# Products with the values for two query heads at once, in a decoder block's attention

## The reference, cut to what matters

```python
N_HEADS = 8; N_KV_HEADS = 2; GQA = 4; HEAD_DIM = 64
WINDOW = 512; Q_BLOCK = 128; SEL_BLOCK = 64; SEL_TOPK = 16
...
s_s = jnp.einsum('bqhgd,bhqsd->bhgqs', qc, ks).astype(f32) * scale + bias_s
p_s = _masked_softmax(s_s, (dist_s >= 0)[:, :, None])
o_s = jnp.einsum('bhgqs,bhqsd->bqhgd', p_s.astype(dtype), vs)
...
s_w = jnp.einsum('bqhgd,bkhd->bhgqk', qc, kw).astype(f32) * scale + bias_w
p_w = _masked_softmax(s_w, valid_w)
o_w = jnp.einsum('bhgqk,bkhd->bqhgd', p_w.astype(dtype), vw)
...
o = g[..., 0:1] * o_cmp + g[..., 1:2] * unblock(o_sel) + g[..., 2:3] * unblock(o_win)
x = x + jnp.concatenate([y_ssm, y_attn], axis=-1) @ w_out[l]
```

## Time and profile before

| | |
|---|---|
| Median of 3 runs | 1084.52 us (1084.23 to 1085.79) |
| Profiled execution | 1085.15 us, its span 1083.3 us |
| TensorE busy | 999.2 us, 92% |
| VectorE busy | 485.3 us, 45% |
| ScalarE busy | 278.5 us, 26% |
| Attention stage | 372 to 597 us of the span |
| Mean granted clock of TensorE | 0.963 of 2.4 GHz |

### The profile page before, as it was taken

How to read it: one execution, slowest core, us unless ns; L and a number is a source line. 1 busy time by engine, 2 the same in 40 slices (tenths; PEclk the granted TensorE clock), 3 DMA queues, 4 the chain that set the end, 5 groups by cost and what they waited for, 6 DMA issues and landing times. The chain is left out here.

```text
span 1083.3 us, 13456 instructions
## 1 busy us (share of the span) xinstructions
PE 999.2 (92%) x5091; PEld 583.5 (54%) x5091; DVE 485.3 (45%) x1213; ACT 278.5 (26%) x629; POOL 149.9 (14%) x146
## 2 busy tenths in 40 slices
PE   6998899989999899999999999996999888989991
PEld 4434687766555466767667455564454333434440
DVE  3444595078635367666665224264651111212115
ACT  3200111131222477656655111020011000101024
POOL 4000000031211212110010000011022101112230
PEclk9999899999999999999999999995999989999996
DMA  9400213040500290000000232536799999999965
GB/s 257 132 15 3 78 25 54 0 45 15 162 1 1 67 251 2 2 1 2 1 2 1 78 135 108 223 141 252 251 308 345 367 396 397 393 393 396 389 212 220
DMA packets 61746, 165.80 MB, mean 153 GB/s; under 512 B 32748, under 2 KB 34860, under 8 KB 49320
## 3 DMA queue, kind: packets, MB, share of 16 engines
q1 hardware_dynamic: 53296, 145.99, 37.8%
q0 software_dynamic: 8096, 18.42, 6.6%
q10 hardware_dynamic: 288, 0.53, 0.1%
HBM read 147.41 MB, written 25.24 MB: 159 GB/s over the span
## 5 line engine op out<-in xcount | busy, mean ns | idle before, releaser
L2001 PE MATMUL banks<-shared,wout 128*64 128x512 f32 (+1 forms) x416 | 149.7, 628 | 13.4 <-issue 11.8
L1609 PE MATMUL banks<-wout,shared 128*128 128x512 f32 x256 | 112.7, 594 | 0.5 <-PEq L1269 0.5
L2001 PEld LDWEIGHTS banks<-shared,wout 128*64 128x64 f32 (+1 forms) x416 | 56.6, 170 | 88.3 <-issue 87.9
L1317 ACT ACTIVATE shared<-shared,low 128x640 f32<-128x640 f32 (+7 forms) x128 | 92.9, 729 | 3.0 <-DVE low L1404 2.5
L2049 DVE SCALAR_TENSOR_TENSOR mix_bt<-mix_bt,slot_coef,banks 128x256 f32<-128x256 f32 x24 | 11.5, 480 | 170.6 <-ACT mix_bt L2029 170.4
L384 PE MATMUL banks<-x,wout 128*128 128x512 f32 x192 | 84.6, 595 | 0.8 <-DVE x L425 0.8
L1367 PE MATMUL banks<-consts,shared 128*128 128x128 f32 x528 | 79.1, 286 | 2.0 <-ACT shared L1317 1.1
L1367 PEld LDWEIGHTS banks<-consts,shared 128*128 128x128 f32 x528 | 56.9, 142 | 41.7 <-issue 36.8
L1609 PEld LDWEIGHTS banks<-wout,shared 128*128 128x128 f32 x256 | 47.6, 190 | 55.2 <-issue 55.2
L2023 PE MATMUL banks<-shared,hidt 128*64 128x512 f32 (+1 forms) x208 | 72.5, 596 | 1.9 <-DVE wout L2064 1.3
L1349 PE MATMUL banks<-shared 64*128 64x512 f32 (+3 forms) x384 | 72.0, 492 | 1.9 <-PEq L988 1.3
(11 more groups left out here) (363 smaller groups left out, 1292.9 us busy)
## 6 DMA issues: line engine op xcount, KB each, us to landing
shared<-in_exp_w_down SPq DMA_DIRECT2D x26, 1024.0 KB, 18.0
shared<-in_exp_w_gate SPq DMA_DIRECT2D x26, 1024.0 KB, 16.7
shared<-in_exp_w_up SPq DMA_DIRECT2D x26, 1024.0 KB, 21.7
x<-in_exp_w_gate SPq DMA_DIRECT2D x6, 1024.0 KB, 16.5
x<-in_exp_w_up SPq DMA_DIRECT2D x6, 1024.0 KB, 24.2
x<-in_exp_w_down SPq DMA_DIRECT2D x6, 1024.0 KB, 25.9
wout<-in_w_in SPq DMA_DIRECT2D x16, 256.0 KB, 5.2
wout<-in_w_in SPq DMA_DIRECT2D x2, 2048.0 KB, 7.9
```

Source lines behind the costliest of these rows:

```text
L1317: nc.scalar.activation(prob[:, u % 2, at:at + n], prob[:, u % 2, at:at + n], ACT.Exp, bias=low[:, u % 2, v, j:j + 1], scale=-1.0, accum_ou ...
L1609: ins = nc.tensor.matmul(psum[n % 4], src[:, i * P:i * P + P], m["wout"][:, k, half * 512:half * 512 + 512], start=k == 0, stop=k == KD - 1)
L2001: ins = nc.tensor.matmul(psum[2 + p][rows].rearrange("p (a f) -> p a f", a=2), xt[:, p, k, rows], wgu[b][:, :, k], start=k == 0, stop=k == ...
```

## The change

The products take two units at once. `pt_pairs` has two pairs of buffers. Unit u writes to half u % 2 of pair u // 2 % 2. The first pair are two pieces of `shared` (the old `pt0` and `pt1`, addressed as the two ends of a view), the second is in `x1`, tiles 4 to 7. A product moves 2 x 128 columns, the same piece of both heads, and writes 256 columns of its bank. `outputs(u - 2)` runs in even iterations only, at the place where it stood, and the last one after the loop. It waits for the last two rounds of both units. The counts that others wait for are halved to fit. Since `x1`'s tiles 4 to 7 are used now, SP loads only the first half of x at the start, waits until all products are done, and then issues the second. The residual add waits for its half at tiles 0 and 4.

```diff
--- before.py
+++ after.py
@@ -1220,7 +1220,7 @@
 
     V = nc.vector
     prob = m["prob"]
-    pt = [m["pt0"], m["pt1"]]
+    pt = m["pt_pairs"]
     low = sb("low", [P, 2, KV, 2])
     mix_coef = sb("mix_coef", [P, 2, HEADS])
     wide = sb("mix_wide", [P, 2, 512])
@@ -1273,7 +1273,11 @@
             for v in range(KV):
                 src = d["w_out"][0, 512 + v * 256:768 + v * 256].rearrange("(i e) n -> e i n", e=HD)
                 sp.dma_start(m["wout"][v * HD:v * HD + HD, 4:8], src).then_inc(m["wout_in"], 16)
-            sp.dma_start(m["x1"][:], d["x"][0].rearrange("(i p) n -> p i n", p=P)).then_inc(m["x_in"], 16)
+            x_back = d["x"][0].rearrange("(i p) n -> p i n", p=P)
+            sp.dma_start(m["x1"][:, 0:4], x_back[:, 0:4]).then_inc(m["x_in"], 16)
+            sp.wait_ge(m["x_in"], 16)
+            sp.wait_ge(pv_done, len(units) // 2)
+            sp.dma_start(m["x1"][:, 4:8], x_back[:, 4:8]).then_inc(m["x_in"], 16)
 
         @block.gpsimd
         def _(gp):
@@ -1302,10 +1306,10 @@
                     eng.wait_ge(o_out, 2 * what - 1 + n0)
                 copy(m["mix_bt"][:, n0], bank[:]).then_inc(t_out[r % 2], 1)
                 return
-            if u >= 2:
-                eng.wait_ge(pv_done, u - 1)
+            if u >= 4:
+                eng.wait_ge(pv_done, u // 2 - 1)
             w = len(what) * P
-            copy(pt[u % 2][:, n0 * P:n0 * P + w], bank[:, 0:w]).then_inc(t_out[r % 2], 1)
+            copy(pt[u // 2 % 2][:, u % 2, n0 * P:n0 * P + w], bank[:, 0:w]).then_inc(t_out[r % 2], 1)
 
         @block.scalar
         def _(act):
@@ -1369,7 +1373,7 @@
 
             def outputs(u):
                 c, i, brs = units[u]
-                for r in of_unit[u][-2:]:
+                for r in of_unit[u][-2:] + of_unit[u + 1][-2:]:
                     pe.wait_ge(t_out[r % 2], r // 2 + 1)
                 if i == 0 and c:
                     for br in brs:
@@ -1382,8 +1386,9 @@
                     for n, kb in enumerate(b):
                         for v in range(KV):
                             half, at = slice(v * HD, v * HD + HD), where[v, j, n]
-                            ins = nc.tensor.matmul(psum[6 + br][half, i * P:i * P + P], vals[:, kb, half],
-                                                   pt[u % 2][:, at * P:at * P + P], start=n == 0, stop=n == len(b) - 1)
+                            ins = nc.tensor.matmul(psum[6 + br][half, i * P:i * P + 2 * P].rearrange("p (h q) -> p h q", h=2),
+                                                   vals[:, kb, half], pt[u // 2 % 2][:, :, at * P:at * P + P],
+                                                   start=n == 0, stop=n == len(b) - 1)
                 ins.then_inc(pv_done, 1)
 
             scores(0)
@@ -1391,10 +1396,10 @@
                 if u + 1 < len(units):
                     scores(u + 1)
                 transposes(u, rounds_of[u][0:2])
-                if u >= 1:
-                    outputs(u - 1)
+                if u >= 2 and u % 2 == 0:
+                    outputs(u - 2)
                 transposes(u, rounds_of[u][2:])
-            outputs(len(units) - 1)
+            outputs(len(units) - 2)
 
         @block.vector
         def _(dve):
@@ -1448,7 +1453,7 @@
                 for r in rounds_of[u][1::2]:
                     evict(dve, V.tensor_copy, r)
                 if u and mixed[u - 1]:
-                    dve.wait_ge(pv_done, u)
+                    dve.wait_ge(pv_done, u // 2)
                     for c, br in mixed[u - 1]:
                         r = mixed_by[c, br][0]
                         dve.wait_ge(t_out[r % 2], r // 2 + 1)
@@ -1669,7 +1674,6 @@
 
     def on_vector(dve):
         chain = Chain(dve, chain_s, m["chained"])
-        dve.wait_ge(m["x_in"], 16)
         dve.wait_ge(m["r_in"], 16 * 8)
 
         def tt(o, a, b, op):
@@ -1680,6 +1684,8 @@
 
         def residual(i, half):
             n = 2 * i + half
+            if half == 0 and i in (0, 4):
+                dve.wait_ge(m["x_in"], 32 if i else 16)
             dve.wait_ge(o_done, n + 1)
             dst = m["x1"][:, i, half * 512:half * 512 + 512]
             V.tensor_tensor(dst, dst, psum[n % 4], ALU.add).then_inc(x_done, 1)
@@ -2552,6 +2558,8 @@
             m["prob"] = part("p (u n) -> p u n", 2 * KV * T, u=2)
             m["oat"] = part("p (b t) -> p b t", 4 * T, b=GQA)
             m["pt1"] = part("p n -> p n", 2 * T)
+            ends = shared[:, 8 * T:24 * T].rearrange("p (h n) -> p h n", h=8)[:, 0:8:7]
+            m["pt_pairs"] = [ends, m["x1"][:].rearrange("p (b t) n -> p b (t n)", t=2)[:, 2:4]]
             fifth = m["x1"][:].rearrange("p a b -> p (a b)")
             m["wgu"] = [shared[:, 4 * T * b:4 * T * b + 4 * T] for b in range(4)] + [fifth[:, 0:4 * T]]
             m["wd"] = [shared[:, 16 * T + 2 * T * b:18 * T + 2 * T * b] for b in range(4)] + [fifth[:, 4 * T:6 * T]]
```

## The result

The changed kernel takes 1102.83 us (median of 4 runs, 1101.26 to 1103.43) against 1085.15 us before (4 runs). The ratio is 1.0175, 95% interval 1.0157 to 1.0193. It is slower, by 17.7 us; forecast were 1101.5 us (1091 to 1108) and +17.0. The profiled execution took 1101.26 us, its span is 1099.4 us.

What follows compares the result with a forecast made beforehand. TensorE was taken to set the attention stage's pace. Saved -7.6, new waits +29.3, old waits -6.7, chunk 0 +0.4, last pair +1.2, reload +0.4: +17.0 us, 1101.5 us against the median of 1084.52, range 1091 to 1108.

Steps and rivals of the forecast that it cites:

- the reload: Before the barrier into the next stage: SP issues the input's second half only after all products, +0.4 us (0 to 0.9).
- the last pair: End of the attention stage: all products of the last two units follow the last unit's copies, +1.2 us.
- The products: TensorE's bursts: ten doubled pairs take 2.26 us where two bursts took 2.49; 21 bursts save 4.7 us.
- The upper bound of 0.43: Cost of a 512-column product, bounding the 256-column cost from above; that end would add 56 us to the sum.
- the case in which wide products are cheap: Rival: 256 columns cost what 128 do, 0.109 us a pair, 28 us less, 1073 us; chance 0.03.
- The waits in odd units: Odd units without products: TensorE waits for the other engines' copies and lows; all new waits 29.3 us, 6.7 of old waits go.
- four rounds: Three odd units: round four waits for VectorE's copy of round two; 2.09, 1.94 and 1.68 us, sum 5.7.
- gates after three rounds: Five odd units ending a chunk: gate round waits for VectorE's copy of round two; 1.13 to 2.15 us each, sum 8.1.
- gates after four: Odd units ending a chunk: gate waits for ScalarE's copy of round three; scores at 4.05 us, chunk 3 at 4.48.
- Chunk 0: Start of the attention stage, partly at 1.2 GHz: its second doubled burst adds 0.4 us (-0.5 to +2).
- chunk 1: Its first pair: 0.7 us for the lows, about 0.6 for VectorE's mix behind longer products; 1.3 us.
- The clock: Rival: gaps in odd units let TensorE's clock fall to 1.2 GHz; 10 us of it cost 5, 1106 us; chance 0.07.

Runs made afterwards that it cites:

- The place alone: Changed kernel with each product moving 128 columns again, both units' products still in the even unit; 1102.8 us, ratio 1.0195 to the kernel before.
- the width alone: Changed kernel with each pair's 256-column burst cut in two, one half in each unit; 1087.19 us, ratio 1.0032 to the kernel before.
- The one with the reload off the path: Changed kernel with its buffer pairs swapped, so SP issues the input's second half one pair earlier; 1101.73 us, ratio 1.0167.
- half bursts: Changed kernel, each 256-column burst split over both units: 1087.19 us; with swapped buffer pairs and ScalarE copying rounds one and two at i = 3: 1080.69 us.
- early copies: ScalarE copies rounds one and two before the exponentials: changed kernel, odd units, 1087.63 us; kernel before, i = 3, 1080.16 us; i = 0 and 3, 1080.79 us.

## Why the prediction was right, point by point

The time, +17.7 against +17.0, and the cause: the two runs that part place and width settle it. The place alone has the whole loss (ratio 1.0195), the width alone a fifth of it (1.0032), in which the reload and the last pair are contained. That the number came within 0.7 us is partly luck: the kernel before had medians of 1082.64 to 1085.15 in its four sets of runs, and several terms of the sum were off in both directions (below).

The products. The 256 columns were taken at 0.216 us a pair of records, 2.26 us a burst of ten. The burst takes 2.31, so that a pair of units saves 0.18 and not 0.22, 1 us less in the sum. The spacing was right: from 405.99 to 407.87 for eight products and from 442.26 to 445.87 for sixteen it is 0.216 each. With the 0.15 of the change that is the measured 2.31. What failed is the 0.05 us behind the first products of a burst, which the sum let go and for which it gave no row. The upper bound of 0.43 came from single records of 512 columns, while 0.109 and 0.216 are pairs; the scores of 512 columns in the earlier trace rows, eight records in 1.92 us (435.22 to 437.14, less the 0.15 of the change), give 0.44 for a pair as well, so the bound holds. The trace refutes the case in which wide products are cheap. The figures of the Trainium skill's page TensorE: Matmul & The Clock Gate, section Back-to-back issue gap, by which twice the columns cost far less than twice the time, do not agree with the 0.109 and 0.216 of this f32 stream.

The waits in odd units, from transposes to scores, forecast and measured: 1.83 against 1.70 with 0.14 more in the scores; four rounds in chunk 3 3.98 and 3.99, in chunk 7 3.83 and 3.83, in chunk 6 3.36 and 3.34; gates after three rounds 3.02, 3.29, 3.57, 3.83 and 3.03, 3.29, 3.57, 3.83; gates after four 4.05 and 4.02. In the window units the prediction named VectorE's lows alone; the trace has an idle time for ScalarE's copy first, and the lows end only some 0.14 us later. This is one of the gates, chunk 5's window branch:

```profile
523.84 1.09 PE L1371 MATMUL banks<-consts,shared 128*128 128x128 f32 x8
...
524.53 0.59 ACT L1312 COPY x<-banks 128x512 f32<-128x512 f32 x1 [1.92 <-PE banks L1371]
...
525.17 0.44 PE L1371 MATMUL banks<-consts,shared 128*128 128x128 f32 x2 [0.24 <-ACT x L1312]
...
526.08 0.69 DVE L1312 COPY x<-banks 128x512 f32<-128x512 f32 x1
...
526.83 0.66 PE L1371 MATMUL banks<-consts,mix_wide 128*128 128x128 f32 x4 [1.22 <-DVE x L1312]
```

It waits 1.22 us for VectorE and takes 3.57 to the scores at 527.41. In the kernel before the same unit takes 3.58 (513.02 to 516.60), with 1.24 us of products in it. There the chain of the lows and the copy had been the pace already, and the unit's products were free.

What was mis-sized. Chunk 3's gates took 4.70, not 4.48. The trace shows the difference: two branches end there, VectorE works out two sets of gate coefficients first, and its lows start 0.45 us after the transposes instead of 0.21. The exponentials, and with them ScalarE's copy of round three, stand 0.13 us later than in chunk 7's unit of the same kind (2.94 against 2.81 us after the transposes). The eight gate transposes take 1.14 us instead of 1.02. Chunk 0 cost 1.0 us instead of 0.4, chunk 1 0.6 instead of 1.35. The granted clock between 384 and 387 us is 0.52 in this trace and 0.94 in that of the kernel before, so the low level lasts longer in chunk 0; whether that is the 0.6 us is not tested. The reload cost 0.6 in place of 0.4: SP issues in 0.37 us, and the next stage starts 0.6 us after that issue has ended; how the barrier uses those 0.6 us the trace does not show.

The clock, a case with a chance of 0.07, came in small, and with it one of the prediction's own signs of being wrong, a new fall in the clock row. The page's row shows it as the digit 7, and so do the timeline and the stretch around it (granted clock 0.72, before the last two columns):

```profile
PEclk9999899999999799999999999996999989999997
```

```profile
423.38 0.66 PE L1371 MATMUL banks<-consts,mix_wide 128*128 128x128 f32 x4 [1.41 <-DVE x L1312]
424.61 1.11 PE L1371 MATMUL banks<-consts,mix_wide 128*128 128x128 f32 x4 [0.57 <-ACT x L1312]
425.65 3.04 PE L1353 MATMUL banks<-shared 64*128 64x512 f32 x8
```

```profile
424.00:430.00 6.00, 5.43 (x25) 3.04 (x26) 1.85 (x4) 1.81 (x5) 0.00 (x0) 0.72 0.01 3
```

Behind two idle times of 1.41 and 0.57 us in chunk 2's last unit the scores of 512 columns take 3.04 us instead of 1.99, and four transposes 1.11 instead of 0.66: 1.5 us more at the 1.2 GHz level. Chunk 2's last unit took 5.67 us from transposes to scores for that reason, where 5.2 was forecast. The kernel before has 0.83 us of idle time in front of the same gate rounds and no fall. The prediction left this out of its sum.

The later stages were to keep their length. From the first scores to the output projection the attention stage grew by 19.3 us, 2.3 more than the sum; clock 1.5, bursts 1.0, chunks 0 and 1 together -0.15, chunk 3 0.2 and reload 0.2 come to 2.75; the 0.45 too much is not placed. The later stages took 2.1 us less in the profiled execution, where the longest stretch of the lower clock is some 3.4 us shorter (748 to 773 us, before 729 to 757), and the earlier ones 1.2 us less. So the profiled execution is 16.1 us longer, and its agreement with 17.0 comes from errors that cancel.

## What to carry to other kernels

An instruction stream that sets the pace may hold work which is free where it stands, since it lies over another engine's chain. Before moving such work count, in each place that it leaves, from what the engine waits for next: here the waits grew by some 22 us for less than 7 us of saved changes (an estimate: the stage's 19.3 us and the 6.6 saved, less clock, reload, last pair and chunk 0). The wider moved operand saved changes between kinds here and no columns.

## What the runs showed of the hardware that I had not expected

TensorE's clock fell now and then in the three versions whose odd units have no products and wait for VectorE's late copy of round two. There TensorE never stood idle for longer than 1.5 us at a time. The profiled run of the changed kernel had one fall to 1.2 GHz between 388 us and the output projection, that of the narrow products at the same place two (at 423 and 570 us). The one with the reload off the path had four, with a granted clock of 0.87 and 0.89 in the two stretches below. The kernel before and the versions with half bursts or with early copies had none between 389 us and the output projection. That the gaps make it fall is argued from this pattern of single traces; no run changes the gaps alone. Six of these seven falls begin within 2 us of an idle time of 1.4 us or more; the one at 554 us does not, and two such idle times in the changed kernel, in front of 438.74 and 569.42, have no fall behind them.

```profile
424.00:462.00 38.00, 34.24 (x210) 20.09 (x212) 20.29 (x50) 19.61 (x48) 3.78 (x4) 0.87 0.00 1
550.00:580.00 30.00, 26.80 (x160) 15.16 (x157) 14.46 (x31) 14.16 (x31) 2.46 (x3) 0.89 0.00 1
```

That run's attention stage was 5.7 us longer than the changed kernel's in spite of the saved reload. Whether such falls also make the time more uneven is not shown: the versions with them spread by up to 9.8 us, but the kernel before spreads by 7.6 us over 29 runs.
